# Routing order ranked before the branch, four tiles of the second expert outside the ring, and scatter matrices by transposes, in a two-block network with a sparse mixture of experts

## The reference

```python
def grouped_moe(h, w_router, router_bias, w_gate, w_up, w_down):
    scores = sigmoid(t @ w_router)              # t: 256 x 1024, 16 experts
    ...
    combine = (one_hot(eidx) * w[..., None]).sum(-2)   # two experts for each token
    for e in range(16):
        he = silu(t @ w_gate[e]) * (t @ w_up[e])        # 1024 x 512 each
        y = y + combine[:, e:e + 1] * (he @ w_down[e])  # 512 x 1024
```

## Time and profile before

| | us |
|---|---|
| median of 3 runs (lowest, highest) | 1593.18 (1592.16, 1597.57) |
| the profiled execution, its own time | 1596.89 |
| its span in the profile | 1595.1 |
| PE busy in the span | 1442.3 (90%) |
| DVE, ACT busy | 955.2 (60%), 670.9 (42%) |
| mean granted clock of the PE | 0.954 |
| DMA: queue of weight tiles | 398.81 MB, 68.8% of 16 engines' time |
| first gather, 32 matmuls | 801.5 to 809.0 |
| first MoE, from the gather to its last matmul | 801.5 to about 1057.7 of the span |
| second MoE | 1325.8 to about 1580 |

### The profile page before, as it was taken

How to read it: one execution, slowest core, us unless ns; L and a number is a source line. 1 busy time by engine, 2 the same in 40 slices (tenths; PEclk the granted TensorE clock), 3 DMA queues, 4 the chain that set the end, 5 groups by cost and what they waited for, 6 DMA issues and landing times.

```text
span 1595.1 us, 27221 instructions
## 1 busy us (share of the span) xinstructions
PE 1442.3 (90%) x10760; PEld 1173.7 (74%) x10760; DVE 955.2 (60%) x1482; ACT 670.9 (42%) x1065; POOL 43.5 (3%) x99
## 2 busy tenths in 40 slices
PE   6999999699999899998899989969999889899994
PEld 6899989459999797986556666649789765566663
DVE  5888857658888744788624443344478853434342
ACT  5444444544444553554234433334355422443331
POOL 3300000000000000000100000000000020000000
PEclk9999999799999899999899999979999989999997
DMA  9899775056999655323269999985533334999995
GB/s 322 285 346 351 272 226 185 1 184 223 351 335 329 211 155 166 109 103 106 106 244 392 413 394 385 391 309 174 153 127 106 106 112 197 409 403 398 394 388 216
DMA packets 159793, 401.96 MB, mean 252 GB/s; under 512 B 6410, under 2 KB 102396, under 8 KB 143324
## 3 DMA queue, kind: packets, MB, share of 16 engines
q1 hardware_dynamic: 158768, 398.81, 68.8%
q10 hardware_dynamic: 380, 1.08, 0.3%
q0 software_dynamic: 560, 0.88, 0.2%
HBM read 399.70 MB, written 1.05 MB: 251 GB/s over the span
## 4 chain that ended last, share of the span: by engine, by line
PE 73%; DVE 14%; ACT 6%; DMA 5%; issue 3%; ACTq 0%; DVEq 0%; SPq 0%
PE bank L1432 14%; PE bank L1311 8%; PE bank L1508 7%; PE bank L1444 6%; PE bank L1516 6%; PE bank L1299 6%; PE bank L1334 5%; PE bank L1567 3%; DMA sb_ring<-in_w_up 3%; PE bank L1360 3%; PE bank L1556 2%; DMA sb_ring<-in_w_gate 2%; PE bank L1582 2%; DVE sb_w_lo L2270 1%; DVE sb_w_lo L2175 1%
## 5 line engine op out<-in xcount | busy, mean ns | idle before, releaser
L1432 PE MATMUL bank<-sb_hT_hi,sb_w_hi 128*128 128x256 f32 x704 | 198.3, 282 | 4.2 <-DVE sb_hT_lo L2152 3.1
L1432 PE MATMUL bank<-sb_hT_lo,sb_w_hi 128*128 128x256 f32 x704 | 196.7, 279 | 0.0
L1432 PE MATMUL bank<-sb_hT_hi,sb_w_lo 128*128 128x256 f32 x704 | 196.4, 279 | 0.0
L2196 DVE TENSOR_TENSOR sb_w_lo<-sb_ring,sb_w_hi 128x1024 fp32r<-128x1024 f32 x128 | 151.2, 1223 | 61.4 <-ACT sb_w_hi L818 61.3
L818 ACT ACTIVATE sb_w_hi<-sb_ring 128x1024 fp32r<-128x1024 f32 x128 | 128.9, 1056 | 115.3 <-PE bank L1432 114.9
L2175 DVE TENSOR_TENSOR sb_w_lo<-sb_ring,sb_proj_hi 128x1024 fp32r<-128x1024 f32 x100 | 117.9, 1220 | 62.3 <-ACT sb_proj_hi L798 62.1
L1508 PE MATMUL bank<-sb_ring,sb_arena 128*32 128x128 f32 (+1 forms) x2304 | 140.4, 321 | 6.7 <-DMA sb_ring<-in_w_gate 5.0
L1432 PEld LDWEIGHTS bank<-sb_hT_hi,sb_w_hi 128*128 128x128 f32 x704 | 132.4, 188 | 6.0 <-issue 4.9
L1311 PE MATMUL bank<-sb_w_lo,sb_hT_hi 128*128 128x256 f32 x480 | 134.8, 281 | 0.0
L1432 PEld LDWEIGHTS bank<-sb_hT_lo,sb_w_hi 128*128 128x128 f32 x704 | 133.4, 189 | 0.7
L798 ACT ACTIVATE sb_proj_hi<-sb_ring 128x1024 fp32r<-128x1024 f32 x100 | 101.0, 1064 | 77.9 <-PE bank L1299 35.0
(11 more groups left out here) (549 smaller groups left out, 2960.5 us busy)
## 6 DMA issues: line engine op xcount, KB each, us to landing
sb_ring<-in_w_up SPq DMA_DIRECT2D x64, 1024.0 KB, 7.4
sb_ring<-in_w_gate SPq DMA_DIRECT2D x64, 1024.0 KB, 7.4
sb_ring<-in_w_down SPq DMA_DIRECT2D x64, 1024.0 KB, 7.9
sb_ring<-in_w_in SPq DMA_DIRECT2D x46, 1024.0 KB, 5.3
sb_ring<-in_ffn_w_in SPq DMA_DIRECT2D x44, 1024.0 KB, 9.2
sb_arena<-in_ada_w SPq DMA_DIRECT2D x32, 1280.0 KB, 6.9
sb_ring<-in_ffn_w_out SPq DMA_DIRECT2D x22, 1024.0 KB, 8.2
sb_ring<-in_w_out SPq DMA_DIRECT2D x12, 1024.0 KB, 4.9
```

What stands on the lines that cost most here:

```text
L1432: ins = mm(bank[4 + 2 * p + b][:, jj * SEQ:(jj + 1) * SEQ], w[wp][:, k, jj * P:(jj + 1) * P], h_parts[hp][:, k, :], start=k == 0 and m == ...
L2196: ins = tt(w_lo[:, slot, c], ring[:, slot, c], w_hi[:, q % 2, c].bitcast(F32), ALU.subtract)
```

## The change

Three parts, all in the MoE.

1. **Order ahead of the branch.** DVE computes the ranking between the steps of `pick`, and the PE's `order_rows` and a new product `counts_by_position` run before the branch, between two halves of `keep_clock`. DVE copies the order row before the second half of `pick`. `slot_no`, `posT`, `sel_r`, `spread`, `pos_copies` and `pos_bc` are gone. A new matrix `valid` (slot number below the count of the expert) multiplies the slot weight.
2. **Four tiles outside the ring.** u0, g0, g1 and u1 of expert 1 go to four free places (three in the arena, one in `xn`), so they wait for no used tile; only the fourth waits for `xn_lo`. The six tiles behind them take the ring slots of expert 0.
3. **`put` by transposes.** `weights(e)` makes two PE transposes of `pick_own` into the same PSUM bank, and DVE copies them to `put`; `gate_up(e)` now waits for that copy (`put`) and no more for `w_slot`.

```diff
+        put_narrow = (view(18432, SEQ), view(7808, SEQ), view(24480, SEQ))
+        ahead = (view(8192, TILE), view(18688, TILE), view(20736, TILE), xn[:, :, :].rearrange("p t d -> p (t d)"))
```

On SP:

```diff
                     e1 = expert_at(1)
-                    load(pos + 6, half(up, e1, 0))
-                    gate_up(1, e1)
+                    ahead_of_ring(0, half(up, e1, 0))
+                    ahead_of_ring(1, half(gate, e1, 0))
+                    ahead_of_ring(2, half(gate, e1, 1))
+                    sp.wait_ge(s["xn_lo"], l + 1)
+                    ahead_of_ring(3, half(up, e1, 1))
```

On the PE, before the branch:

```diff
-                keep_clock(4)
+                keep_clock(2)
+                order_rows(l, bank[3])
+                counts_by_position(l, bank[7])
+                keep_clock(2, bank[6])
...
+            def counts_by_position(l, out):
+
+                pe.wait_ge(s["ranking"], 3 * l + 2)
+                mm(out[:, 0:NE], ones[0:NE, :], turned_count[0:NE, :], start=True, stop=True).then_inc(s["ranking_rows"], 1)
```

On the PE, in `weights(e)` and behind it:

```diff
+                    pe.wait_ge(s["pick_own"], TURN * i + (NE * l + e + 1))
...
                     for t in range(T):
-                        if e:
-                            ins = mm(bank[4][:, 0:1], pick_own[:, t, :], comb[:, t, bass.ds(TURN * i + e, 1)], start=t == 0, stop=t == T - 1)
...
+                        mm(bank[4][:, 0:1], pick_own[:, t, :], own_weight, start=t == 0, stop=t == T - 1)
+                    for t in range(T):
+                        ins = tr(bank[4][:, SEQ + t * P:SEQ + (t + 1) * P], pick_own[:, t, :], ident[:, :])
                     ins.then_inc(s["w_psum"], 1)
...
                 def gate_up(e, i=0):
 
-                    pe.wait_ge(s["w_slot"], TURN * i + (NE * l + e + 1))
+                    pe.wait_ge(s["put"], TURN * i + (NE * l + e + 1))
...
                 down(0)
-                spread(0)
                 rows("u0", 1, bank[5], 0)
-                spread(1)
```

On DVE, in `weights(e)`, behind the branch, and in the routing:

```diff
                     v.wait_ge(s["w_psum"], TURN * i + (NE * l + e + 1))
-                    cp(w_slot, bank[4][:, 0:1]).then_inc(s["w_slot"], 1)
+                    tt(w_slot, bank[4][:, 0:1], valid[:, bass.ds(TURN * i + e, 1)], M).then_inc(s["w_slot"], 1)
+                    cp(put[:, :] if e in WIDE else put_narrow[e % TURN], bank[4][:, SEQ:2 * SEQ]).then_inc(s["put"], 1)
...
-                puts(0)
                 product(1)
...
+                link(v.tensor_tensor_reduce(above, key, ident[:, 0:NE], 1.0, 0.0, M, AD, own_key))
                 v.tensor_reduce(own2[:, 0, :], rows3(own), AX.X, ALU.max)
+                link(ts(above, key, own_key, None, ALU.is_gt))
+                v.tensor_reduce(own2[:, 1, :], rows3(own), AX.X, AD)
+                v.tensor_tensor_reduce(counted, off_f[:, 1, :], ident[:, 0:NE], 1.0, 0.0, M, AD, own_off)
+                link(v.tensor_reduce(own_rank, above, AX.X, AD))
+                ts(turned_order, ranks[:, 2, :], own_rank, None, ALU.is_equal).then_inc(s["ranking"], 1)
                 link(tt(own2[:, 2, :], own2[:, 1, :], own2[:, 0, :], ALU.subtract))
                 for t in range(T):
                     ins = ts(pick[:, t, :], slot_row, own2[:, 0, t:t + 1], None, ALU.is_equal)
                 link(ins)
+                v.wait_ge(s["ranking_rows"], 2 * l + 1)
+                cp(order_i[0:1, :, :].rearrange("p a e -> p (a e)"), bank[3][0:1, 0:2 * NE]).then_inc(s["order"], 1)
                 for t in range(T):
                     ins = stt(pick[:, t, :], slot_row, own2[:, 2, t:t + 1], pick[:, t, :].bitcast(F32), ALU.is_equal, AD)
                 ins.then_inc(s["routed"], 1)
+                link(v.tensor_tensor_reduce(counted, count, ident[:, 0:NE], 1.0, 0.0, M, AD, own_count))
+                v.wait_ge(s["ranking"], 3 * l + 1)
+                ts(turned_count, turned_order, own_count, None, M).then_inc(s["ranking"], 1)
```

More of the change, by code:

```diff
@@ L407, in build, with in_moe, is_ahead, ring_at @@
         block = ctx.enter_context(nc.Block())
+        def in_moe(pos):
+            return [pos - place[f"moe.{l}"] for l in range(LAYERS) if 0 <= pos - place[f"moe.{l}"] < 6 * NE]
+        def is_ahead(pos):
+            return any(RING <= rel < RING + AHEAD for rel in in_moe(pos))
+        def ring_at(pos):
+            assert not is_ahead(pos)
+            return pos - AHEAD * sum(pos >= place[f"moe.{l}"] + RING + AHEAD for l in range(LAYERS))
+        def before_in_slot(pos):
+            return pos - RING - (AHEAD if any(RING + AHEAD <= rel < 2 * RING + AHEAD for rel in in_moe(pos)) else 0)
         def slot_view(pos, kind):
-            w = ring[:, pos % RING, :]
+            if is_ahead(pos):
+                return ahead[in_moe(pos)[0] - RING].rearrange("p (k n) -> p k n", n=kind)
+            w = ring[:, ring_at(pos) % RING, :]
             if kind == 3 * QL:
@@ L877, in expert_input, with first_window @@
                       bias=modp[:, 0, k:k + 1]).then_inc(s["xg_act"], 1)
+                def first_window():
+                    act.wait_ge(s["routed"], l + 1)
+                    act.wait_ge(s["w_psum"], NE * l)
+                    A(pick_own.rearrange("p t (a s) -> p t a s", s=HALF),
+                      pick[:, :, 0:HALF].bitcast(F32).unsqueeze(2).broadcast_to([P, T, P // HALF, HALF]),
+                      ACT.Copy).then_inc(s["pick_own"], 1)
                 def window(e, i=0):
@@ L922, in ye_high @@
                     ins.then_inc(s["ye_hi"], 1)
-                def pos_copies(b):
-                    for n in range(4):
-                        act.wait_ge(s["pos_bc"], 8 * l + 4 * b + n + 1)
-                        A(pos_bc[:, 8 * b + 2 * n:8 * b + 2 * n + 2, :], two[n], ACT.Copy).then_inc(s["pos_out"], 1)
                 def wide(e, i=0):
@@ L1243, in _, with landed @@
             mm, tr = pe.matmul, pe.transpose
-            def landed(pos, i=0):
-                pe.wait_ge(ring_full[pos % RING], 16 * i + 16 * (pos // RING + 1))
+            def landed(pos, i=0, step=1):
+                if is_ahead(pos):
+                    pe.wait_ge(ahead_full, 16 * AHEAD * sum(pos >= place[f"moe.{l}"] for l in range(LAYERS)))
+                    return
+                at = ring_at(pos)
+                pe.wait_ge(ring_full[at % RING], 16 * step * i + 16 * (at // RING + 1))
             PARTS = ((0, 0), (0, 1), (1, 0))
@@ L1691, in ada_turn, with keep_clock @@
                 ins.then_inc(s["ada_turned"], 1)
-            def keep_clock(n):
+            def keep_clock(n, out=bank[7]):
                 for _ in range(n):
-                    mm(bank[7][:, :], ones[:, :], x[:, 0, 0:512], start=True, stop=True)
+                    mm(out[:, :], ones[:, :], x[:, 0, 0:512], start=True, stop=True)
             def gate_rows(run, out):
@@ L2015, in _ @@
                 with pe.If(fits_ < 1):
-                    order_rows(l, bank[3])
+                    pe.wait_ge(s["ranking"], 3 * l + 3)
                     for t in range(T):
@@ L2169, in split @@
             def split(name):
-                pos, j = place[name], split_no[name]
+                slot, j = ring_at(place[name]) % RING, split_no[name]
                 for half in range(2):
@@ L2368, in sparse @@
                 quarter(15)
-                puts(NE - 1)
             quarters = [0]
```

158 lines of the change are left out of this document (62 added, 96 removed).

## The result

| | before | after |
|---|---|---|
| median of 6 runs each, us | 1593.94 | 1627.08 |
| lowest, highest | 1592.16, 1602.21 | 1622.34, 1632.12 |
| recorded ratio, 95% interval | | 1.0191 (1.0166 to 1.0216) |
| profiled execution, its span | 1596.89, 1595.1 | 1630.32, 1628.6 |
| mean granted clock | 0.954 | 0.948 |

A forecast was written before the change was run, and what follows sets the result against it. It took the wide experts' turn of 47.3 us as bound by the PE, ACT and DVE chain or, narrowly, DMA. Per layer 1.75 + 1.5 + 0.2 = +3.4, +6.9 in two, gave 1593.18 + 6.9 = 1600 us; range 1587 to 1610.

The forecast's parts named there:

- The gather: Start of the gather behind the branch in each MoE layer: later by 3.3 to 4.9 us, taken as +4.1.
- (a): Ahead of the gather: ranking 0.85 us and order copy 0.17 before the end of `pick`, which ends near 801.5.
- (b): Ahead of the gather: `own_count` and `turned_count` 0.45 us, then the PE's counts product 0.3, reaching 802.2.
- (c): Ahead of the gather: four `keep_clock` rows, 1.84 us at full clock, up to 3.4 at low; then 0.7 to the gather.
- 1.03 us behind `pick`: Reading of the kernel before: the gather starts at 801.50, 1.03 us after `pick` ends at 800.47.
- The loads: Four early tiles leave 10 us earlier in the first layer; gain 1.05 us a layer, the rest has no one waiting.
- The gather at 1.2 GHz: Rival: low clock through the gather's 32 matmuls, up to 6 us more a layer, 1608 to 1612; chance 0.07.
- Experts 0 and 1: First experts' path: 2.81 us of removed steps, 1.01 added for transposes, window read and the `put` copy.
- Turns +0.5 each: Each turn to the last wide expert: +0.75 where the chain bounds, +0.25 where g0's tile is late, mean +0.5.
- Behind it the queue is full and hides the rest: Layer's end, after d0 of the last wide expert is freed: tiles always queued, so nothing further is added.
- In a span whose earlier part is unchanged: Expected sign: u0 of the first wide expert about 2 us later than 847.9, with nothing moved earlier in the span.
- DMA as the bound: Rival: DMA bounds the MoE, so streams starting 10 us earlier in each layer give 1573 us; chance 0.14.

The follow-up runs named there:

- e3: Changed kernel without the second pair of `keep_clock` products ahead of the branch; the gather started 14.2 us behind the counts; its time is not given.
- e9: Changed kernel, arena on a multiple of 512 bytes, early loads held until the gather began, order row first behind the branch, counts' product behind the gather: 1598.70 us (1.0018).
- e10: e9 with the loads outside the ring held until the gather is done: 1597.90 us (1.0007).
- e17: e3 with the loads outside the ring held until the gather has begun; gather 2.9 and 2.4 us earlier than in e3; its time is not given.
- e5: Changed kernel, arena at its old place, early loads held until the gather began, counts' product moved behind the gather: 1611.48 us (1.0068).
- e16: Changed kernel with only the products around the branch reordered: order row (so the loads) behind the branch, counts' product behind the gather: 1606.24 us (1.0076).

## Why the prediction was wrong

The way was forecast, slower, and the order ahead of the branch was priced as the largest loss; its size was off by half, and two other losses had no term.

- **The gather, "I take +4.1"**: it was +7.5 and +7.3, and this is the step that failed first. (a) and (b) were right on DVE: `pick` ended 6.4 us behind the counts, `turned_count` 6.7. (c) failed, "Four of the eight rows of `keep_clock`: 1.84 us at full clock", up to 3.4, "then 0.7 us to the gather": with 0.3 for the product, 2.9 to 4.5 us from `turned_count` to the gather. It measured 7.4 (810.53 to 817.93). What stands there is not `keep_clock`, whose rows e3 took out without moving the gather, but the code of the branch: 2.0 us from `turned_count` to the packet, 2.8 more for the tiles ahead of it, 2.6 from the packet's start to the first product. The 0.7 was read from the second layer, where the packet had started 2.1 us before `keep_clock` ended. The reading that the gather started "1.03 us behind `pick`" hid the same thing: before the change, too, it started 1.6 us behind the packet's end, and `pick` had been ready.
- **The loads, "no one waiting for it"**: that the early loads are worth little was right; not even the 1.05 us a layer could be seen (e9, e10). That it can cost was not priced: the four tiles held the branch's code for 2.4 to 2.9 us a layer (e17 against e3). The prediction counted SP's queue and not who else uses the DMA engines.
- **"The gather at 1.2 GHz", chance 0.07**: this happened in part, 5.6 us of the gather at half clock in the first layer and 3.4 in the second, which is 2.8 and 1.7 us of time and not 6. Against it stood 2.46 us of idle at full speed; here the clock fell in a gap of 3.03 us with half as many `keep_clock` rows ahead.
- **"Experts 0 and 1", -2.81 + 1.01**: right. In e5, and alike in e9 and e16, from expert 0's first product to the down product of expert 1 are 24.94 us where 26.79 stood: -1.85. The copy of `put` took 0.41 us in all 32 cases, as the row said, and not the 0.70 of the prediction's other figure.
- **Turns +0.5 each**: right in the mean, with some luck in it. The transposes were taken at 0.22 a pair and measured 0.26 to 0.29, and 0.37 us that no term had came with them, so g0 to the next u0 is 0.89 longer and not 0.44. But u0 to g0 of a wide expert, 8.18 us at the low clock, was 6.6 to 7.6 in many turns of the changed kernels, the form for which the prediction had 6.35 without the transposes. The whole turn is +0.64, three of them +1.9 where +1.5 was forecast.
- **"Behind it the queue is full and hides the rest"**: the end of a layer is not only DMA's; the products behind the last tile run at 1.2 or 2.4 GHz, 4 us apart.
- **"In a span whose earlier part is unchanged"**: a term put at nothing without a reason. 128 bytes ahead of the arena cost 6.6 us in the kernel before, and 9 to 11 of the 33 go with the place in the changed one.
- **DMA as the bound** fell: with the gather in its old place and tiles 8 us earlier nothing was gained.

The sum as measured: 18 to 21 us for what was put ahead of the branch (with its fetch and clock) and 9 to 11 for the place. The small rest is an estimate from the traces: 4 for six turns and 4 to 5 for the more frequent late ends, less 3 for the first experts. That is 32 to 38 in all, against 30 to 33.

## What to carry to other kernels

Treat a branch as an instruction with a cost of its own. A wait for another engine's result ahead of it delays the fetch of the code (4.7 us a layer here), while products already queued run beside the fetch. Large transfers started before it delay it further, so start them behind it. When a tensor is added ahead of others, keep the old addresses or test the place as an experiment of its own. And where the last tiles are waited for, look at the clock of the products behind them.

## What was not expected of the hardware

The gather behind the taken branch came 2.5 to 3.1 us after the start of a 16 KB instruction packet and 1.5 to 1.7 us after its end, in both layers of every trace, and the packet started 2.7 to 2.8 us later with four weight tiles in the engines (e3 against e17). The cadence of products (256 columns) changed from a mean of 117.45 to 119.40 ns when operands moved by 128 bytes, with nearly the same histogram in different programs; with the arena at 119296, a multiple of 512 bytes, the gaps are even, 116 to 120 ns (only this one such place was tried). The Trainium skill (SBUF — State Buffer, "Operand start alignment") asks only for a multiple of the element's size and says that this is about legality, not speed; all four places satisfy it and their times differ by up to 0.8%.
